# Transposes inside the triangular inverses written as 64x64 identity products, copied together with the level's product

## The reference, cut to what matters

```python
lmat = jnp.where(strict, jnp.einsum('bhncd,bhnsd->bhncs', kb, k) * decay, 0.0)
rhs = jnp.concatenate([vb, kb * jnp.exp(gc)[..., None]], axis=-1)
sol = lax.linalg.triangular_solve(lmat, rhs, left_side=True, lower=True, unit_diagonal=True)
```

## Time and profile before

| | us |
|---|---|
| Median of 3 runs | 3795.48 |
| Lowest and highest run | 3793.31, 3803.53 |
| The profiled execution, its own time | 3804.48 |
| Its span, first to last instruction | 3803.2 |
| PE busy in the span | 3532.9 (93%) |
| DVE, ACT, POOL busy | 1675.3, 1181.9, 1393.0 |

### The profile page before, as it was taken

How to read it: one execution, slowest core, us unless ns; L and a number is a source line. 1 busy time by engine, 2 the same in 40 slices (tenths; PEclk the granted TensorE clock), 3 DMA queues, 4 the chain that set the end, 5 groups by cost and what they waited for, 6 DMA issues and landing times.

```text
span 3803.2 us, 72363 instructions
## 1 busy us (share of the span) xinstructions
PE 3532.9 (93%) x31740; PEld 2276.7 (60%) x31740; DVE 1675.3 (44%) x2942; ACT 1181.9 (31%) x2157; POOL 1393.0 (37%) x1239
## 2 busy tenths in 40 slices
PE   7999899999999989898999998999888888889998
PEld 3755584344554555554555554456667677658887
DVE  1245562366531234444333425524666666433344
ACT  3154342322214633413000002114666556320002
POOL 1230550133312245665323333344444444144443
PEclk9999899999999989999999999999999999999999
DMA  5441005311112135301111211331000000122221
GB/s 190 133 137 34 2 14 178 127 47 54 49 49 68 45 111 177 134 23 52 59 56 56 66 51 50 105 112 51 17 17 17 17 17 3 55 70 89 89 89 67
DMA packets 196435, 263.78 MB, mean 69 GB/s; under 512 B 6135, under 2 KB 151671, under 8 KB 194072
## 3 DMA queue, kind: packets, MB, share of 16 engines
q1 hardware_dynamic: 188960, 241.74, 19.2%
q10 hardware_dynamic: 7160, 17.41, 1.2%
HBM read 246.55 MB, written 12.58 MB: 68 GB/s over the span
## 4 chain that ended last, share of the span: by engine, by line
PE 53%; ACT 6%; DVE 4%; issue 4%; POOL 1%; DMA 0%; ACTq 0%; DVEq 0%; SPq 0%; POOLq 0%
PE ps L238 42%; PE ps L3238 2%; PE ps L771 2%; ACT mem L848 1%; PE ps L382 1%; PE ps L798 1%; PE ps L786 1%; PE ps L489 1%; DVE mem L829 1%; PE ps L3757 1%; POOL mem L3540 0%; PE ps L498 0%; PE ps L3765 0%; ACT mem L858 0%; ACT mem L3173 0%
## 5 line engine op out<-in xcount | busy, mean ns | idle before, releaser
L238 PE MATMUL ps<-mem 64*64 64x64 f32 (+4 forms) x25120 | 2624.0, 295 | 98.4 <-ACT mem L3173 26.1
L238 PEld LDWEIGHTS ps<-mem 64*64 64x64 f32 (+1 forms) x25120 | 1704.2, 150 | 1025.4 <-issue 519.6
L3103 POOL TENSOR_TENSOR mem<-mem 128x256 f32<-128x256 f32 (+1 forms) x264 | 228.2, 878 | 342.6 <-ACT mem L3650 176.8
L866 POOL TENSOR_SCALAR mem<-mem 128x768 f32<-128x768 f32 (+2 forms) x128 | 219.3, 1727 | 202.7 <-DVE mem L832 202.7
L2366 ACT ACTIVATE mem<-ps 128x384 f32<-128x384 f32 (+1 forms) x80 | 35.7, 446 | 779.1 <-PE ps L238 736.8
L2353 POOL TENSOR_TENSOR mem<-mem 128x512 f32<-128x512 f32 (+1 forms) x80 | 100.9, 1261 | 445.2 <-PE ps L238 368.4
L596 POOL TENSOR_TENSOR mem<-mem 128x512 f32<-128x512 f32 (+1 forms) x72 | 75.3, 1064 | 417.5 <-ACT mem L591 414.3
L2377 DVE TENSOR_TENSOR mem<-mem,ps 128x384 f32<-128x384 f32 (+1 forms) x80 | 39.9, 499 | 415.8 <-PE ps L238 415.8
L3238 PE MATMUL ps<-mem 128*128 128x128 f32 x960 | 166.4, 289 | 26.6 <-DVE mem L3162 14.0
L3162 DVE TENSOR_TENSOR mem<-mem,ps 128x256 f32<-128x256 f32 (+1 forms) x220 | 109.6, 514 | 110.8 <-PE ps L238 109.9
L3171 ACT ACTIVATE mem<-ps 128x256 f32<-128x256 f32 (+1 forms) x220 | 101.5, 462 | 173.3 <-PE ps L3238 173.0
(11 more groups left out here) (339 smaller groups left out, 4082.7 us busy)
## 6 DMA issues: line engine op xcount, KB each, us to landing
mem<-i_mod_w SPq DMA_DIRECT2D x48, 1024.0 KB, 6.9
mem<-i_ffn_wg SPq DMA_DIRECT2D x22, 1024.0 KB, 5.3
mem<-i_ffn_wu SPq DMA_DIRECT2D x22, 1024.0 KB, 5.3
mem<-i_e_w_in SPq DMA_DIRECT2D x16, 1024.0 KB, 6.2
mem<-i_o_w_in SPq DMA_DIRECT2D x16, 1024.0 KB, 5.4
mem<-i_ffn_wd SPq DMA_DIRECT2D x16, 1024.0 KB, 4.9
mem<-i_e_mod_w SPq DMA_DIRECT2D x12, 1024.0 KB, 11.8
mem<-i_o_mod_w SPq DMA_DIRECT2D x12, 1024.0 KB, 6.6
```

The lines of the kernel that those rows point to most:

```text
L238: ins = e.h.matmul(out, l, r, start=(i == 0), stop=(i == n - 1))
L866: K.pool.h.tensor_scalar(w, w, stat(i, o, 1), None, MUL).then_inc(*nm.up(tag, i, o))
L3103: K.pool.h.tensor_tensor(m3(self.slot(l)), self.lraw, bm(C(K, f"cm{self.d}", l, 64), 2 * self.np), MUL).then_inc(*self.mk.up(key, l))
```

## The change

In `Inverse64`, the transposes of a level become products of U's 64x64 blocks with a 64x64 identity (`turned`), by the same `many`, order and placing as the product p, into columns 256 and up of the same banks b and b+1. There is no signal "v" and no bank `tb`. ACT copies both, transposed U and p, by one operation into one tile PT (P is its first half, T its second). The second product reads them by `by_half`. The sixth level of the delta scan is treated alike: eight 64x64 products, one copy, no scaling by -1; instead the strengths are negated once into NB (48 columns) and used in the last multiplication. In the delta scan the banks are renamed: GB = 5 holds the gates alone, and kk goes to TB = 4, which `first` of both lanes also uses. The three multiplications that read kk stand one step earlier on DVE. The RWKV scan has the class change alone.

```diff
@@ delta_scan
-    RI = [{"U": w[0], "T": w[1], "P": w[2], "Lm": w[3:5]} for w in own]
+    RI = [{"U": w[0], "Lm": w[3:5]} for w in own]
+    for R, m in zip(RI, (held, tail)):
+        R["PT"] = m[:, 256:768]
...
-    TB, FB, KB, UB = 4, 5, 6, 7
+    TB, GB, KB, UB = 4, 5, 6, 7
...
-        K.pe.h.matmul(K.ps[FB], C(K, "ones"), gm[d], start=True, stop=True).then_inc(*pr.up(d, i, "gate"))
-        K.busy[FB] = [(ux, (d, i, "x"))] + ([(ex, (d, i, "qs"))] if x else [])
+        K.pe.h.matmul(K.ps[GB], C(K, "ones"), gm[d], start=True, stop=True).then_inc(*pr.up(d, i, "gate"))
+        K.busy[GB] = [(ux, (d, i, "x"))] + ([(ex, (d, i, "qs"))] if x else [])
         yield from idle(2)
-        vacant(K, FB)
+        vacant(K, TB)
         for h in range(4):
-            ins = K.pe.h.matmul(K.ps[FB][:, HS[h]], kT[:, h, c0:c0 + 128], kT[:, h, c0:c0 + 128], start=True, stop=True)
+            ins = K.pe.h.matmul(K.ps[TB][:, HS[h]], kT[:, h, c0:c0 + 128], kT[:, h, c0:c0 + 128], start=True, stop=True)
         ins.then_inc(*pr.up(d, i, "kk"))
-        K.busy[FB] = [(ux, (d, i, "L"))]
+        K.busy[TB] = [(ux, (d, i, "L"))]
@@ front_dve
-        yield from idle(2)
+        yield from idle(1)
         K.dve.wait_ge(*pr.at(d, i, "kk"))
...
-        yield from idle(5)
+        yield from idle(6)
@@ inverse_pe
-        yield from inv.levels(a, TB)
-        vacant(K, TB)
+        yield from inv.levels(a)
+        claim(K, a, inv.cp, inv.key, 6)
         K.pe.wait_ge(*inv.u.at(inv.key, 5))
-        turn(K, K.ps[TB], U, 0, 2).then_inc(*inv.pr.up(inv.key, "v", 6))
-        K.busy[TB] = [(inv.cp, (inv.key, "T", 6))]
-        vacant(K, a)
+        for g in range(2):
+            for h in range(2):
+                w = slice((2 * g + h) * 64, (2 * g + h) * 64 + 64)
+                K.pe.h.matmul(K.ps[a + 1][on(h), on(g)], U[on(q), w], K.id64[on(q), :], start=True, stop=True)
@@ inverse_act
-        K.act.wait_ge(*inv.pr.at(inv.key, "v", 6))
-        K.act.h.activation(RI[d]["T"], K.ps[TB][:, 0:256], ACT.Copy).then_inc(*inv.cp.up(inv.key, "T", 6))
         K.act.wait_ge(*inv.pr.at(inv.key, "p", 6))
-        K.act.h.activation(RI[d]["P"][:, 0:128], K.ps[2 * d][:, 0:128], ACT.Copy, scale=-1.0).then_inc(*inv.cp.up(inv.key, "P", 6))
+        K.act.h.activation(h3(inv.P), K.two(2 * d)[:, :, 0:128], ACT.Copy).then_inc(*inv.cp.up(inv.key, 6))
@@ delta_scan, before the lanes
+    K.dve.h.tensor_scalar(NB, BE, -1.0, None, MUL).then_inc(*ux.up("NB"))
@@ Inverse64
+    def turned(self, b):
+
+        return self.K, self.np, BY_EH, by_rows(self.K, b, "heads", 64, 256), (chunky(self.R["U"]), lambda i, e, h: self.id64[64 * e:64 * e + 64, :])
+
+    def levels(self, b):
+
+        K, key, R, n = self.K, self.key, self.R, self.np
         for l in range(1, 6):
-            vacant(K, tb)
+            claim(K, b, self.cp, key, l)
             K.pe.wait_ge(*self.u.at(key, l - 1))
-            turn(K, K.ps[tb], R["U"], 0, self.np).then_inc(*self.pr.up(key, "v", l))
-            K.busy[tb] = [(self.cp, (key, "T", l))]
-            claim(K, b, self.cp, key, "P", l)
+            many(*self.turned(b))
             K.pe.wait_ge(*self.mk.at(key, l))
-            many(K, self.np, BY_EH, by_rows(K, b, "heads"), (chunky(self.slot(l)), chunky(R["U"]))).then_inc(*self.pr.up(key, "p", l))
+            many(K, n, BY_EH, by_rows(K, b, "heads"), (chunky(self.slot(l)), chunky(R["U"]))).then_inc(*self.pr.up(key, "p", l))
             yield
             claim(K, b, self.u, key, l)
-            K.pe.wait_ge(*self.cp.at(key, "P", l))
-            many(K, self.np, BY_HE, by_rows(K, b, "chunks"), (heady(R["T"]), heady(R["P"]))).then_inc(*self.pr.up(key, "u", l))
+            K.pe.wait_ge(*self.cp.at(key, l))
+            many(K, n, BY_HE, by_rows(K, b, "chunks"), (by_half(self.T, n), by_half(self.P, n))).then_inc(*self.pr.up(key, "u", l))
             yield
...
-            K.act.wait_ge(*self.pr.at(key, "v", l))
-            K.act.h.activation(self.R["T"][:, 0:self.n], K.ps[turned][:, 0:self.n], ACT.Copy).then_inc(*self.cp.up(key, "T", l))
             K.act.wait_ge(*self.pr.at(key, "p", l))
-            K.act.h.activation(split(self.R["P"], n), both(K, b, n), ACT.Copy).then_inc(*self.cp.up(key, "P", l))
+            out = self.R["PT"][:, 0:n * 256].rearrange("p (a h w) -> p h a w", h=2, w=n * 64)
+            K.act.h.activation(out, K.two(b).rearrange("p h (a w) -> p h a w", w=256)[:, :, :, 0:n * 64], ACT.Copy).then_inc(*self.cp.up(key, l))
```

More of the change, by code:

```diff
@@ L1359, in delta_scan @@
     held = K.ring.slots[K.ring.slot(first + 2)]
-    own = [[m[:, i * 256:(i + 1) * 256] for i in range(7)] for m in (held, K.alloc(1792))]
+    tail = K.alloc(1792)
+    own = [[m[:, i * 256:(i + 1) * 256] for i in range(7)] for m in (held, tail)]
     more = [K.alloc(512) for _ in range(2)]
-    RI = [{"U": w[0], "T": w[1], "P": w[2], "Lm": w[3:5]} for w in own]
+    RI = [{"U": w[0], "Lm": w[3:5]} for w in own]
+    for R, m in zip(RI, (held, tail)):
+        R["PT"] = m[:, 256:768]
     Lc, Lo, OD = [(own[d][5], more[d][:, 0:256]) for d in range(2)], [(own[d][6], more[d][:, 256:512]) for d in range(2)], ot[:, 4:8, :]
@@ L1367, in delta_scan @@
     ub, qs, rt = ([xs[4 * c + 2 * d:4 * c + 2 * d + 2] for d in range(2)] for c in range(3))
-    S = K.rows
+    S, NB = K.rows, K.a3(6, 8)
     gate, scl = K.sig("un_gate", "pool"), K.sig("un_scale", "pool")
@@ L1385, in inverse @@
     def inverse(d, i):
-        return Inverse64(K, ("dn", d, i), ("dn", d, i - 1) if i else None, RI[d], d, d, m3(Lc[d][i % 2]), 2, K.id64, TB, TB)
+        return Inverse64(K, ("dn", d, i), ("dn", d, i - 1) if i else None, RI[d], d, d, m3(Lc[d][i % 2]), 2, K.id64, TB)
     def strength(d, tt, rows, n):
@@ L1444, in front_act @@
                 K.act.wait_ge(*ch.at(d, i - 2, "o"))
-            K.act.h.activation(qs[d][i % 2], K.ps[FB], ACT.Exp).then_inc(*ex.up(d, i, "qs"))
+            K.act.h.activation(qs[d][i % 2], K.ps[GB], ACT.Exp).then_inc(*ex.up(d, i, "qs"))
         yield
@@ L1494, in inverse_pe @@
         ins.then_inc(*inv.pr.up(inv.key, "p", 6))
-        K.busy[a] = [(inv.cp, (inv.key, "P", 6))]
         yield
         claim(K, a, ux, d, i, "off")
-        K.pe.wait_ge(*inv.cp.at(inv.key, "P", 6))
+        K.pe.wait_ge(*inv.cp.at(inv.key, 6))
         for g in range(2):
             for h in range(2):
-                ins = K.pe.h.matmul(K.ps[a + h][on(q), on(g)], T[on(h), (2 * g + q) * 64:(2 * g + q) * 64 + 64], P[on(h), on(g)], start=True, stop=True)
+                ins = K.pe.h.matmul(K.ps[a + h][on(q), on(g)], inv.P[on(h), 128 + 64 * g:192 + 64 * g], inv.P[on(h), on(g)], start=True, stop=True)
         ins.then_inc(*inv.pr.up(inv.key, "u", 6))
@@ L3079, with __init__ @@
 class Inverse64:
-    def __init__(self, K, key, before, R, lane, d, lraw, np_, id64, first=None, turned=None):
+    def __init__(self, K, key, before, R, lane, d, lraw, np_, id64, first=None):
         self.K, self.key, self.before, self.R, self.lane, self.d = K, key, before, R, lane, d
-        self.fb, self.tb = first, turned
+        self.fb = first
+        self.P, self.T = (R["PT"][:, j * np_ * 128:(j + 1) * np_ * 128] for j in range(2))
         self.lraw, self.np, self.n, self.id64 = lraw, np_, np_ * 128, id64
@@ L3133, in pe @@
         yield from self.first(b + 1)
-        yield from self.levels(b, b + 2)
+        yield from self.levels(b)
     def pool(self, ready):
@@ L3189, in chunky, with by_half @@
     return lambda i, e, h: ap[64 * e:64 * e + 64, ((p0 + i) * 2 + h) * w + at:((p0 + i) * 2 + h) * w + at + n]
+def by_half(ap, n):
+    return lambda i, e, h: ap[64 * h:64 * h + 64, (e * n + i) * 64:(e * n + i) * 64 + 64]
 def heady(ap, p0=0):
@@ L3282, in __init__ @@
             L.update({"kk": sc(1024), "lr": sc(1024), "L": w[:, 1024 * d:1024 * d + 512], "rb": w[:, 1024 * d + 512:1024 * d + 1024]})
-            L.update({n: sc(512) for n in ("k", "bt", "U", "T", "P")})
-            L.update(Lm=[sc(512), sc(512)], kkt=L["kr"][:, 0:NT], rt=L["kr"][:, NT:NT + NX], tk=L["P"])
+            L.update({n: sc(512) for n in ("k", "bt", "U")}, PT=sc(1024))
+            L.update(Lm=[sc(512), sc(512)], kkt=L["kr"][:, 0:NT], rt=L["kr"][:, NT:NT + NX], tk=L["PT"][:, 0:512])
         self.YC = [sc(NX) for _ in range(2)]
```

16 lines of the change are left out of this document (7 added, 9 removed).

## The result

The changed kernel takes 3830.04 us (median of 4 runs, 3825.51 to 3832.97) against 3796.27 for the kernel before on the same chip: ratio 1.0085, interval 1.0067 to 1.0103. It is slower by 34 us, outside the predicted range. The profiled execution has a span of 3830.4 us, 27.2 more than before, at the same mean clock (0.972).

A forecast was written before the change was run, and what follows sets the result against it. PE's fixed order, often waiting behind ACT or DVE, was taken as the bound. RWKV -8, delta turns -5 and -2, stall +9.4 and +0.3, gate bank -1.3: -6.6 us, from 3795.5 to 3789; range 3775 to 3806.

The forecast's parts named there:

- the price of the identity products in RWKV's four-head levels: RWKV four-head levels: 32 records at 15 ns take 0.49 us where transposes took 0.58, giving PE 0.22 us a turn.
- Nothing is gained: ACT is late next: RWKV lone four-head level: 3.84 us becomes 3.83, as ACT's copies then set the pace; four heads together 0.8 us gained.
- RWKV, two heads: RWKV two-head levels beside a finish: 1.0 us gained a pair of heads, 7.0 us over seven pairs.
- The first half: RWKV's two-head pair without a finish: five levels of about 0.07 us gained, 0.35 us in all.
- Delta, turns: Delta scan's identity products: 0.54 us gained a dense unit, 5 us over nine units, 2 us more at beginning and end.
- Delta, bank TB: Delta scan, kk in TB: `first` waits 1.18 us a unit for kk's readers; +9.4 us dense, +0.3 in a thin unit.
- Rival 2: Delta scan: the stall before `first` is covered by PE's other work; 16 us gained, 3779 us; chance 0.25 with a cheaper copy.
- the 1.3 forecast: Delta scan's start: with the gates in their own bank, `first` comes about 1.3 us earlier.
- The delta scan as a whole: All delta scan terms, from turns, the stall at kk's bank and the gates' own bank: -5-2+9.4+0.3-1.3.
- Rival 4: Levels' merged copy costs as much as the two, wholly after the product: +21 us, 3817 us; chance 0.17.
- The bound of 1.20: Merged copy of 1024 columns: upper bound 1.20 us if two banks in one operation cost as two; 1.04 taken.
- Rival 3: Both scans: PE bounds everything, so all turns give their 0.22 us; -34 us with the stall, 3761 us; chance 0.08.

The follow-up runs named there:

- e_rw4_late: Kernel before with the change in RWKV's two-head levels only; four-head levels keep transposes and two copies, both waiting for the product: 3819.65 us, ratio 1.0052 to before.
- e_merged: Changed kernel with 128x128 transposes again at levels 1 to 5 of both scans, still copied with the product by one operation: 3818.72 us, ratio 1.0046 to before.
- e_best: Changed kernel with RWKV's four-head levels as before and kk in the gates' bank: 3798.99 us, ratio 0.9988 to before.
- e_merged4_gb: Changed kernel with transposes and one copy in RWKV's four-head levels alone, kk in the gates' bank: 3803.18 us, ratio 1.0012 to before.
- e_kk_gb: Changed kernel with kk back in the gates' bank and its three readers at their old step: 3827.42 us, ratio 1.0067 to before.
- e_dn_old: Changed kernel with the whole delta scan of before; the change stays in RWKV alone: 3836.26 us, ratio 1.0093 to before.
- e_pad1: Kernel before plus 32 unread four-column matmul records in each lane's four-head level of RWKV: 3839.15 us, ratio 1.0102 to before.
- e_pad2: Kernel before plus 64 unread four-column matmul records in each lane's four-head level of RWKV: 3948.95 us, ratio 1.0391 to before.
- e_rw4_turn: Changed kernel with RWKV's four-head levels put back to transposes and two copies: 3801.98 us, ratio 1.0001 to before.
- e_best2: Changed delta scan with kk in the gates' bank, whole RWKV scan with the levels of before: 3792.92 us, ratio 0.9983 to before.
- e_rw_old: Changed kernel with all RWKV levels put back to transposes and two copies; delta scan stays changed: 3801.08 us, ratio 0.9998 to before.

## Why the prediction was wrong

**The step that failed** is the price of the identity products in RWKV's four-head levels: "32 x 15 ns = 0.49", with bounds of 0.24 and 0.45 for the smaller case, all of them times on the array. The 15 ns hold (61 records from 3281.26 in 1.15 us). But each of the 28 records more per lane and level is two instructions, and instructions come 256 at a time every 3.5 to 4.0 us. I divided the time of the earlier trace rows by their engine work and never by their instructions: 136 records in 3.84 us is about what the supply gives at best. The lone four-head level, forecast at 3.83, became 5.5 to 5.8. The warning stood in the earlier trace rows, "<-issue 21.1" behind the copy's 26.1, and I passed it over as if it were nothing.

**A second, smaller error** in the same step: "Nothing is gained: ACT is late next" put the copy's lateness at zero, by letting both lanes' products end sooner. With transposes it costs 0.49 a level and 8 to 10 us in all (`e_rw4_late`, `e_merged`). What it would cost with identity products and instructions in time was not run.

**The split, timed.** Three runs differ in the four-head levels alone, with the same changed delta scan (kk in the gates' bank) and the same two-head levels; each ratio is to the kernel before on its own chip. With the levels of before it is 0.9988 (`e_best`), with transposes and one copy 1.0012 (`e_merged4_gb`), with identity products and one copy 1.0067 (`e_kk_gb`); the three intervals do not overlap. So the late copy is worth 0.0024, about 9 us, and the records are worth 0.0055, about 21 us. Single traces spread more: with the same code in the four-head halves these take 231.0 us in the changed kernel, 221.0 in `e_dn_old` and 218.7 in `e_kk_gb`, and the lower clock is granted for 17.1, 3.4 and 6.8 us of them. So part of the 32.8 us is the clock's, and not of the mechanism. Each of its low stretches in the changed kernel's halves begins within 2.2 us of a stop's end; that the stops bring them about is not shown.

**RWKV, two heads:** forecast 1.0 us a pair of heads, measured 0.3 to 0.8 (20.9 to 21.4 for 21.7; the last, 21.7, nothing). The first half was forecast at -0.35 and lost 3.4, with a stop of 3.34 us and 6.8 us of lower clock in it. All eight together gained nothing, against the 7.35 forecast.

**Delta, turns:** forecast 0.54 a dense unit; the change without the stall gives 0.91, of which the products instead of transposes are 0.74. Right in sign, too small.

**Delta, bank TB:** forecast 1.18 us a unit, measured 1.20, from the place and the releaser named. Rival 2 falls. Over the scan the change of bank costs 5.7 us (213.0-207.3), less than the 9.4, since with the gates in a bank of their own the second gate product follows the first after 3.54 us (388.48 to 392.02) where it took 6.92 (388.26 to 395.18), and by the third the changed kernel is 1.6 us ahead, for the 1.3 forecast. The forecast kept the clock of that start at 0.65; from 388 to 424 it was 0.78 in the changed kernel and 0.67 in `e_kk_gb`, so part of the lead may be the clock's. The delta scan as a whole: forecast +1.4 (-5-2+9.4+0.3-1.3), measured -3.1.

**The rivals.** Rival 4 had the sign, and with 3817 came nearest, but its mechanism is refuted: the merged copy measured 1.02 us and decided nothing by its length. The prediction said that no row shows two banks in one operation. The earlier trace rows do: the product lies in banks b and b+1, and its copy (line 3173) reads both, in the 0.386 and 0.604 us that the transposes' copy takes from one bank. The bound of 1.20 had no ground. Rival 3, PE as the bound, was rejected because the earlier trace rows show it waiting for ACT; it was near its bound all the same, in instructions and not in array time.

## What to carry to other kernels

Count PE's instructions as a resource of its own: in a stretch of short float products, two instructions a record, compare the number of records with the time, at 128 records in about 3.7 us as measured here, before replacing one large instruction by many small ones. Idle time in the middle of a run of products with no releaser, at equal counts of records, is this limit. And where one copy replaces two, look at what the first of them used to be hidden beneath.

## What the runs showed of the hardware

PE's instructions are fetched in blocks of 16 KB, 256 instructions or 128 records: the packets of queue q8 follow the records through all kernels (31740 records and 250 packets; 34300 and 270 in `e_pad1`; 36860 and 290 in `e_pad2`; 36012 and 283 after). Where PE waits for them in the changed kernel's last four-head half, a block takes 3.47 to 4.02 us, which is 27 to 31 ns a record against the 15 ns in which the array gets through one. In none of the fourteen traces do two packets of this queue start less than 3.2 us apart.

The packets' own times show what fills the 3.7 us. Behind the stops of over 0.4 us in RWKV the next packet starts 1.05 us or more after PE has started again (median 1.15 us over the changed kernel's 48), takes 0.9 to 1.4 us in that last half, and PE starts again 1.2 to 1.6 us after its end. Such stops in the other traces give the same two figures, 1.05 us or more and 1.2 to 1.6 us. So while PE is short of instructions, the fetch of a block is not seen to begin before PE has started on the one before. 128 records of 15 ns are 1.9 us and end before the next block is there.

A record of a 64x64 or 64x4 product takes 15 ns at the upper level of the clock and 28 ns at the lower (`e_pad2`), so that at the lower level 128 records take 3.6 us by the array alone.

The Trainium skill, "Runtime: NRT & Kernel Launch", Instruction fetch mechanics, says that an engine's instruction store is refilled in blocks of 16 KiB, 256 instructions, and that the fetch is hidden since instructions are issued more slowly than they arrive. The size agrees with the runs. That it is hidden does not: 48 stops, 50.2 us, stand in the RWKV scan of the changed kernel.

The time between the halves is 292 to 296 us in some kernels and 300 to 301 in others, with the same code there. Part of this goes with the clock: the lower level was granted there for none of 292.0 us in `e_rw4_turn`, for 6.8 of 294.7 before and 6.8 of 293.8 after, and for 20.5 of 300.4 in `e_best2` and of 301.4 in `e_dn_old`. It is not the whole, since `e_rw_old` has 296.0 and `e_kk_gb` 300.3 with 10.2 each. What lowers the clock, and whether the rest hangs on where the borders of the blocks fall, stays open.
